# Tile 0's expert search taken head by head, in a fused attention, state-space and retrieval layer

## The reference

```
q = (rmsnorm(x) @ w_query)                      # 8 heads x 2 halves x 128
s = einsum('thcd,hckd->thck', q, keys)          # 128 scores per head and half
top_s, top_i = top_k(s, 16)
cand_s = top_s[0][:, None] + top_s[1][None, :]  # 16 x 16 sums per head
best_s, best_j = top_k(cand_s, 16);  idx = cand_i[best_j]
gate = softmax(best_s)
act  = gelu(einsum('thkd,td->thk', u_table[idx], x))
y    = einsum('thk,thkd->td', gate * act, v_table[idx])
```

## Time and profile before

| | us |
|---|---|
| median of the runs | 3525.19 |
| the profiled execution | 3523.02 |
| its span | 3521.2 |
| PE busy | 2364.3 (67%) |
| DVE busy | 2222.2 (63%) |
| POOL busy | 1322.6 (38%) |
| ACT busy | 1010.7 (29%) |
| gathers (L1372) | 1088, 1140.92 MB, 79.8% of the DMA engines' span |

### The profile page before, as it was taken

The page is one execution under the profiler, slowest core; times in us unless marked ns, Lnnn a source line. Parts: engine busy times, 40 slices in busy tenths (PEclk is TensorE's granted clock), DMA queues, the critical chain, the costliest instruction groups (busy, mean ns, idle before and its releaser), DMA issues.

```text
span 3521.2 us, 35625 instructions
## 1 busy us (share of the span) xinstructions
PE 2364.3 (67%) x9377; PEld 967.5 (27%) x9377; DVE 2222.2 (63%) x5008; ACT 1010.7 (29%) x3384; POOL 1322.6 (38%) x1229
## 2 busy tenths in 40 slices
PE   6997654476568566856685677567756765676676
PEld 3554434142114111411141124113311321241121
DVE  5344235557856775687568656855795578568754
ACT  2121211232333223233322332232233323332222
POOL 0010300344444444434444444444444434444442
PEclk9998777797688778967896778678867886897799
DMA  4111241699999999999999999999999999999998
GB/s 159 57 55 53 50 161 54 286 412 415 385 392 421 415 385 400 412 412 388 408 416 406 390 405 417 398 385 421 417 388 399 417 407 384 415 419 417 390 422 346
DMA packets 192652, 1212.96 MB, mean 344 GB/s; under 512 B 28952, under 2 KB 35416, under 8 KB 51688
## 3 DMA queue, kind: packets, MB, share of 16 engines
q0 software_dynamic: 156672, 1140.92, 79.8%
q1 hardware_dynamic: 35416, 69.28, 5.7%
q10 hardware_dynamic: 320, 0.07, 0.0%
HBM read 1194.51 MB, written 15.55 MB: 344 GB/s over the span
## 4 chain that ended last, share of the span: by engine, by line
DMA 29%; PE 22%; DVE 16%; issue 12%; ACT 5%; POOL 2%; DVEq 0%; SPq 0%; POOLq 0%; ACTq 0%; PEldq 0%
DMA uv_ring<-in_uv_table,idx 28%; PE ACC L1790 13%; PE TQ L1745 7%; DVE uv_ring L1633 5%; DVE S L1597 2%; DVE picks L1598 2%; DVE S L1596 2%; POOL uv_ring L1372 2%; ACT dg L1466 1%; ACT dot L1459 1%; PE OP L1726 1%; DMA wq<-in_w_query 1%; ACT dot L1449 1%; DVE dot L1633 0%; DVE pos L1528 0%
## 5 line engine op out<-in xcount | busy, mean ns | idle before, releaser
L1790 PE MATMUL ACC<-uv_ring,dg 128*64 128x512 f32 x4352 | 1472.8, 788 | 919.0 <-ACT dg L1466 918.3
L1372 POOL DMA_INDIRECT uv_ring<-in_uv_table,idx x1088 | 1258.3, 1157 | 1807.0 <-PE ACC L1790 1357.0
L1633 DVE CUSTOM_DVE_ANT_0 uv_ring<-uv_ring,xn 128x1024 f32<-128x1024 f32 x1088 | 1325.0, 1226 | 791.7 <-DMA uv_ring<-in_uv_table,idx 728.9
L1790 PEld LDWEIGHTS ACC<-uv_ring,dg 128*64 128x64 f32 x4352 | 343.7, 167 | 1930.8 <-ACT dg L1466 1396.9
L1449 ACT ACTIVATE dot<-dot 128x2 f32<-128x2 f32 x544 | 110.5, 203 | 1749.2 <-DVE dot L1633 1748.9
L1466 ACT ACTIVATE dg<-stack,dot 128x64 f32<-128x64 f32 x1088 | 327.8, 341 | 53.0
L1745 PEld LDWEIGHTS TQ<-glu_and_queries,wq 128*128 128x128 f32 x2304 | 266.4, 194 | 66.3 <-issue 64.7
L1745 PE MATMUL TQ<-glu_and_queries,wq 128*128 128x128 f32 x2304 | 280.5, 280 | 1.4 <-DMA wq<-in_w_query 1.2
L1459 ACT ACTIVATE dot<-gate,dot 128x1 f32<-128x1 f32 x1088 | 261.2, 287 | 17.7
L507 PE MATMUL PJ<-w_in,xT 128*128 128x512 f32 (+1 forms) x432 | 158.7, 528 | 1.5 <-DMA w_in<-in_w_in 1.5
L507 PEld LDWEIGHTS PJ<-w_in,xT 128*128 128x128 f32 x432 | 82.9, 192 | 79.2 <-issue 74.0
(11 more groups left out here) (319 smaller groups left out, 1653.2 us busy)
## 6 DMA issues: line engine op xcount, KB each, us to landing
uv_ring<-in_uv_table,idx POOLq DMA_INDIRECT x1088, 10.8
glu_and_queries<-in_w_glu SPq DMA_DIRECT2D x9, 1024.0 KB, 17.1
wq<-in_w_query SPq DMA_DIRECT2D x1, 8192.0 KB, 33.1
xt<-in_x SPq DMA_DIRECT2D x9, 512.0 KB, 3.4
xr<-scratch_x SPq DMA_DIRECT2D x9, 512.0 KB
w_in<-in_w_in SPq DMA_DIRECT2D x2, 2048.0 KB, 10.8
xk<-in_x SPq DMA_DIRECT2D x8, 512.0 KB, 3.2
scratch_x<-xk SPq DMA_DIRECT2D x8, 512.0 KB, 2.6
```

What stands on the lines that cost most here:

```text
L1372: pool.indirect_dma_start(out=ring[:, s_ % RING, :], out_offset=None, in_=a["uv_table"], in_offset=bass.IndirectOffsetOnAxis(ap=idx[:, s_: ...
L1633: V.tensor_tensor_reduce(row, row, xn[:, g, :], 1.0, 0.0, ALU.mult, ALU.add, dot[:, s_:s_ + 1]).then_inc(dots, 1)
L1790: ins = nc.tensor.matmul(ACC[GT * g:GT * (g + 1), b, :], dg[:, n % DG, :], ring[:, n % RING, D + 512 * b:D + 512 * b + 512], start=False, ...
```

## The change

- Tile 0 is a turn of its own, `first`, outside of the loop, which now runs tiles 1 to 6.
- Of tile 0's preparation only heads 0 to 2 of the step list (to xn_next and its transposes) run as before. Queries and scores are taken head by head on PE and ACT, one head's copy beside the next one's matmuls. DVE takes head 0 through its pieces A (two best16 of 128), B (62 candidates and their search), C and C2 (the match, in quarters, and the exchange to idx), then A of heads 1 to 3, then D of head 0 (the gates), and then products. The other pieces stand behind products of tile 0: head e's B at slot 3, 11, 20, 29, 38, 52, 66 (e = 1 to 7), C two slots later, C2 three, D five; A of heads 4 to 7 at slots 10, 18, 27, 36.
- POOL waits in tile 0 for an index semaphore once a head, ACT for gates once a head, and ACT takes one Exp for each head.
- Tile 1's whole preparation and the steps (0,*) of tile 2 run in slots 3 to 127 of tile 0: two steps a slot in slots 3 to 18, then some 1.03 a slot.
- In all tiles the exchange of numbers and gates is made by DVE, eight instructions on 64 partitions at step (7,13), which is slot 109; the matmul of picks at (7,14) is gone.
- w_query is laid out by head and loaded in eight transfers of 1 MB, the first of them ahead of keys, place and spread; stack and g_fin come last.

```diff
+        def first_steps(s_):
+            lo = LEAD + KS
+            return max(0, 2 * (s_ - LEAD)) if s_ < lo else 2 * KS + (s_ - lo) * (NSLOT - KS) // (NSLOT - lo)
+            if turn == "first":
+                lo, hi = first_steps(s_), first_steps(s_ + 1)
+                return [(1 + i // NSLOT, i % NSLOT // KS, i % KS) for i in range(lo, hi)]
+        BEST_AT = {1: 3, 2: 11, 3: 20, 4: 29, 5: 38, 6: 52, 7: 66}
+        FIRST_HEADS = {at + n: (e, piece) for e, at in BEST_AT.items() for n, piece in ((0, "B"), (2, "C"), (3, "C2"), (5, "D"))}
+        FIRST_HEADS |= {10: (4, "A"), 18: (5, "A"), 27: (6, "A"), 36: (7, "A")}
...
+                sp.dma_start(wq[:, 0].rearrange("p k n -> p (k n)"), a["w_query"][0]).then_inc(wq_in[0], 16)
...
+                for e in range(1, EH):
+                    sp.dma_start(wq[:, e].rearrange("p k n -> p (k n)"), a["w_query"][e]).then_inc(wq_in[e], 16)
-                sp.dma_start(wq[:], a["w_query"].rearrange("(k p) n -> p k n", p=P)).then_inc(weights, 16)
...
+                        if turn == "first" and s_ % KS == 0:
+                            pool.wait_ge(first["idx"], s_ // KS + 1)
...
+                def first_gates(e):
+                    act.wait_ge(first["nmax"], e + 1)
+                    A(ex[:, e, :], best[:, e, :], ACT.Exp, bias=nmax[:, e:e + 1],
+                      accum_out=esum[:, e:e + 1]).then_inc(first["ex"], 1)
...
-                        k["picked"].mark(V.tensor_tensor(ex, ex, bcast(esum[:], KS, 2), ALU.mult))
+                            k["gate_ready"].mark(take_gates(0, EARLY // KS))
+                            k["idx_ready"].mark(take_picks(0, EARLY // KS))
...
+                def first_head(e, piece):
+                    head, i = slice(e, e + 1), 2 * (e % 4)
+                    if piece == "A":
+                        dve.wait_ge(first["S"], e + 1)
+                        for n in range(2):
+                            best16(top_v[:, e, n, :], top_i[:, e, n, :], S[:, i + n, :])
+                        dve.sem_inc(first["topped"], 1)
+                    elif piece == "B":
+                        dch_(V.tensor_copy(top_f[:, head], top_i[:, head]))
+                        dch_(V.tensor_scalar(top_f[:, head, 0, :], top_f[:, head, 0, :], float(KEYS), None, ALU.mult))
+                        pairwise(top_v[:, head], first_cand, ALU.add)
+                        dch_(pairwise(top_f[:, head], first_cid, ALU.add), True)
+                        best16(best[:, e, :], pos[:, e, :], first_cand[:, 0, :])
+                        V.tensor_copy(pos_f[:, e, :], pos[:, e, :])
+                        dch_(V.tensor_scalar(nmax[:, head], best[:, e, 0:1], -1.0, None, ALU.mult))
+                        dve.sem_inc(first["nmax"], 1)
+                    elif piece in ("C", "C2"):
+                        n = KS // 4
+                        for k0 in range(0, KS // 2, n) if piece == "C" else range(KS // 2, KS, n):
+                            dch_(V.tensor_tensor(quarter[:], bcast(place[:], n, 1), bcast(pos_f[:, e, k0:k0 + n], NCAND, 2),
+                                                 ALU.is_equal))
+                            dch_(V.tensor_tensor(quarter[:], quarter[:], first_cid[:].to_broadcast([P, n, NCAND]), ALU.mult))
+                            dch_(V.tensor_reduce(idx_f[:, e, k0:k0 + n], quarter[:], AX.X, ALU.add))
+                        if piece == "C2":
+                            take_picks(e, e + 1).then_inc(first["idx"], 1)
+                    else:
+                        dve.wait_ge(first["ex"], e + 1)
+                        dch_(V.reciprocal(esum[:, head], esum[:, head]))
+                        take_gates(e, e + 1).then_inc(first["gate"], 1)
...
+                for piece in ("A", "B", "C", "C2"):
+                    first_head(0, piece)
+                for e in range(1, 4):
+                    first_head(e, "A")
+                first_head(0, "D")
+                for s_ in range(LEAD):
+                    product(0, s_)
...
+                retrieve("first", 0)
+                with dve.Fori(1, PT - 1) as t:
```

More of the change, by code:

```diff
@@ L1451, in weigh @@
                 def weigh(t, s_):
-                    if s_ == 0:
+                    if isinstance(t, int) and t == 0:
+                        if s_ % KS == 0:
+                            act.wait_ge(first["gate"], s_ // KS + 1)
+                    elif s_ == 0:
                         k["gate_ready"].of(act, t)
@@ L1482, in retrieve @@
                             diagonal(t, s_)
-                            if prep := prepared(turn, t, s_):
+                            if turn == "first" and FIRST_HEADS.get(s_, ("", ""))[1] == "B":
+                                first_gates(FIRST_HEADS[s_][0])
+                            for prep in prepared(turn, t, s_):
                                 prepare(*prep)
@@ L1614, in take_early @@
[L1614 to L1619, removed]
+                        if isinstance(t, int) and t == PT:
+                            k["gate_ready"].mark(take_gates(0, EH, 1))
+                            k["idx_ready"].mark(take_picks(0, EH, 1))
+                        else:
+                            k["gate_ready"].mark(take_gates(0, EARLY // KS))
+                            k["idx_ready"].mark(take_picks(0, EARLY // KS))
@@ L1653, in retrieve @@
                 def retrieve(turn, t):
-                    turn_now[0] = t
+                    turn_now[0] = None if turn == "first" else t
                     for s_ in range(LEAD, slots_of(turn)):
                         product(t, s_)
-                        if s_ == KS - 4 and turn != "samples":
+                        if s_ == KS - 4 and turn in ("steady", "eighth"):
                             take_rest(t)
-                        if s_ == TAKE and turn != "samples":
-                            take_early(t + 1)
-                        if prep := prepared(turn, t, s_):
+                        if turn == "first" and s_ in FIRST_HEADS:
+                            first_head(*FIRST_HEADS[s_])
+                        for prep in prepared(turn, t, s_):
                             prepare(*prep)
@@ L1679, in _ @@
                             dve.wait_ge(bottom, 16 * 2)
-                        elif (h, j) == (3, 0):
-                            dve.wait_ge(weights, 16 * 6)
                         prepare(0, h, j)
[L1683 to L1689, removed]
+                for piece in ("A", "B", "C", "C2"):
[3 more added lines that the diff above has]
+                first_head(0, "D")
+                dve.wait_ge(weights, 16 * 2)
+                for s_ in range(LEAD):
+                    product(0, s_)
+                for n in ("topped_a", "topped_b", "nmax_done", "idx_ready", "gate_ready", "idx_rest", "gate_rest"):
+                    dve.sem_inc(k[n].sem, 1)
+                retrieve("first", 0)
+                dch.loop_begins(1)
+                with dve.Fori(1, PT - 1) as t:
                     retrieve("steady", t)
@@ L1758, in prepare, with first_queries, first_scores, spread_rows @@
                         k[f"s_{n}"].mark(ins)
[L1759 to L1766, removed]
-                    k["xn_done"].of(pe, t)
[L1769 to L1773, removed]
+                def first_queries(e):
+                    pe.wait_ge(wq_in[e], 16)
+                    if e >= 2:
+                        pe.wait_ge(first["qT"], e - 1)
+                    for i in range(2):
+                        for n in range(KD):
+                            ins = nc.tensor.matmul(TQ[:, e % 2, i * P:(i + 1) * P], wq[:, e, n, i * QH:(i + 1) * QH],
+                                                   xnT[:, n, :], start=(n == 0), stop=(n == KD - 1))
+                    ins.then_inc(first["q"], 1)
+                def first_scores(e):
+                    pe.wait_ge(first["qT"], e + 1)
+                    if e >= 2:
+                        pe.wait_ge(first["S"], e - 1)
+                    if e == 0:
+                        pe.wait_ge(keys_in, 16 * 3)
+                    for i in range(2):
+                        ins = nc.tensor.matmul(ZS[:, e % 2, i * KEYS:(i + 1) * KEYS], qT[:, 2 * (e % 4) + i, :],
+                                               keys[:, 2 * e + i, :], start=True, stop=True)
+                    ins.then_inc(first["s"], 1)
+                def spread_rows(t, g):
+                    k["xn_done"].of(pe, t)
+                    for b in range(2):
+                        ins = nc.tensor.matmul((OP, TQ)[g][:, b, :], spread[:, g, :],
+                                               xn_next[:, 512 * b:512 * b + 512], start=True, stop=True)
+                    k[f"xn_spread_{'ab'[g]}"].mark(ins)
                 def begin(t):
@@ L1811, in _ @@
                 pe.wait_ge(early, 48)
-                for h in range(EH):
+                for h in range(3):
                     for j in range(KS):
@@ L1815, in _ @@
                             pe.wait_ge(bottom, 16 * 2)
```

(19 more changed lines are left out.)

123 lines of the change are left out of this document (83 added, 40 removed).

## The result

The changed kernel takes 3501.37 us (3497.77 to 3503.19), a ratio of 0.9928 [0.9914, 0.9943] to the kernel before: 24 us faster by the medians, where 52 were forecast. The profiled execution has a span of 3495.9, 25.3 less than before. Of the executions used further down, one with useless work early took 4522.55 us; it is in no ratio, and without it that kernel's median is 3516.95 and not 3517.28.

A forecast was written before the change was run, and what follows sets the result against it. DMA was taken to bound the experts' stage, with tile 0's search an idle hole before it. First product 81 us earlier, less 27 excess in tile 0, less 4 for the handover, gave 50: forecast 3473 us, range 3446 to 3503.

The forecast's parts named there:

- the sum was 54 us at product 128: Tile 0: first product 81 us earlier, less 27 us of excess up to product 128, a gain of 54.
- the term of DVE's idle time: Tile 0: 84.4 us of added DVE work set against 107 us idle, 28 of it after slot 80.
- First product 81 earlier: Before tile 0's products: head 0 alone goes first, so the first product comes at 566.7 against 647.91.
- Second half of xn by 567.5: Start of tile 0: the copy of the second group of rows ends by 567.5, before product 1 needs it.
- Slots 3 to 18, 19 over: Tile 0: 9 us work excess plus 12.5 of waits for PE and ACT (bounds 0 and 25), less 2.5 overlap.
- Slots 19 to 49, 4 over: Tile 0: 37.3 us of added DVE work against 36.4 idle; 4 us taken as excess.
- Slots 50 to 80, 4 over: Tile 0: 19.6 us of added DVE work against 19.4 idle; 4 us taken as excess.
- After slot 81, none: Tile 0 from slot 81: time as before, 127.8 us.
- The +4 for the handover: Seven tiles and the samples: exchange moved from slot 116 to 109, about 0.7 us a tile slower, +4 in all.
- That ACT's table loads are hidden: Tile 0: 14 table loads, 18 us on ACT, hidden by the ring's cycle: cost 0, or 5 us.
- The rival of stalls at double pace, 3500: Tile 0: double-pace preparation stalls PE, ACT and DVE, 25 us, pieces cost 10 in each later stretch; 3500, chance 0.10.

The follow-up runs named there:

- useless work early: Changed kernel plus 32 useless DVE comparisons of 248 elements, two behind each product of tile 0's slots 19 to 34: 3517.28 us, ratio 0.9976.
- even pace: Changed kernel with tile 0's 144 preparation steps spread evenly, 1.15 a slot over slots 3 to 127, not two a slot in 3 to 18: 3485.13 us, 0.9891.
- The two kernels with useless work: Changed kernel plus 32 useless DVE comparisons in tile 0, behind products of slots 19 to 34 (3517.28 us, 0.9976) or 111 to 126 (3504.81 us, 0.9949).

## Why the prediction was wrong

The mechanism was right: the hole before the first gather closes, and DVE's search inside tile 0 gives part of it back. Its size was not: the sum was 54 us at product 128, measured were 26. (The step from there to 3473 has a slip of its own: 50 less than the median of 3525.2 is 3475.) The step that failed is the term of DVE's idle time: it was taken as span less busy, and as larger still. By steps:

- **First product 81 earlier: 77.6.** I read the row of 128 query matmuls in the earlier trace rows as 16 groups of eight. It shows two records for each matmul, so it holds four heads of 16, and a head takes 3.74 us, not 1.8. Head 0's took 5.57, with the granted clock at 0.67 of full speed from 536.2 to 541.8. Pieces A to D of head 0 took 26.9 us with the pieces A of heads 1 to 3 between them, for 25.7 forecast; the instructions of a quarter took 0.42 us, 0.45 from start to start, as forecast.
- **Second half of xn by 567.5: 580.** The same error eight times over: a head takes PE 4.75 us, not 3. The wait of 8.6 made products 0 to 3 take 12.1 us. Before they took 8.2: 3.9 lost.
- **Slots 3 to 18, 19 over: 23.7.** The three waits were 6.5, 2.7 and 5.8 for 5 to 6, 2.5 and 4.5. This was the step best foreseen, and even pace shows that it counts in full.
- **Slots 19 to 49, 4 over: 10.9.** I named no wait here, though step (2,6) waited 3.1 for OP before too; here it took 4.5, and rows 6.6.
- **Slots 50 to 80, 4 over: 15.7.** The step that failed most. I took span less busy time, 79.0 - 59.6, as time that a piece can use. But tile 1's searches are there, and a search of 128 holds DVE 1.98 us, of which 1.57 are busy (first line below): nothing entered the gaps of its five chained instructions. 31 products at 1.15 and 15.5 searches at 1.98 are 66.3 of 80.2: 13.9 were free for 19.6 of work, and 3.9 and 4.8 of waits for S and rows came on top.
- **After slot 81, none: 2.7 won.**

Together 3.4 + 3.9 + 4.7 + 6.9 + 11.7 - 2.7 = 28. Nor is a product counted as 1.22 + 0.08 in the busy time, for which I had added 5 us of idle time to each stretch: three in a row after the change, from 580.18 to 583.62, are busy 3.44 of 3.44 us. The view of before held a better measure of free time, DVE's waits for rows in the stretches of the earlier trace rows. A window for DVE over one search, then these waits in 656.1:698.6, 698.6:778 and 778:857:

```profile
558.12:560.10 1.98, 1.57 (x9) 1.00 0.00 0
...
DVE uv_ring L1633 <- DMA uv_ring<-in_uv_table,idx: 18.6, 15, 2.6
DVE uv_ring L1633 <- DMA uv_ring<-in_uv_table,idx: 33.9, 26, 2.1
DVE uv_ring L1633 <- DMA uv_ring<-in_uv_table,idx: 9.4, 15, 1.4
```

Idle time was 19.4, 36.4 and 19.4 there: only in the last stretch is it twice the waits for rows. Added work less these waits is 28.2 - 18.6, 37.3 - 33.9 and 19.6 - 9.4. With the new or longer waits of after (15.0; 1.4 for OP and 6.6 for rows; 1.6 for S and 4.8 for rows) this makes 24.6, 11.4 and 16.6, where 23.7, 10.9 and 15.7 were measured. The two kernels with useless work agree with that: work is free where DVE waits for rows, and costs nearly its length where it doesn't.

The +4 for the handover can't be read from the changed kernel: its lead is 26.0 at product 128, 28.4 at product 256 and 25.3 at the end, and identical code of the later tiles varies by 13 from profile to profile. Alone the exchange did cost, but the stated reason isn't supported. That ACT's table loads are hidden held, to 3 us, and no run shows the search held by the ring or by PE's clock of 0.71 to 0.79. The rival of stalls at double pace, 3500, is nearest to the total, with 54 us over where 51.5 were measured, but that is in part luck: it had 34 in slots 3 to 18, which took 23.7, and 20 in the two later stretches, which took 26.6, and it missed 3.4 at the first product and 3.9 at the second.

## What to carry to other kernels

Time that an engine has free beside a stream of transfers is not span less busy: take its waits for the stream, stretch by stretch. Or price each piece by start to start in a row where it stands in a chain, add the products by theirs, and compare with the rate of the transfers. When work is moved beside a stream, halving the distance between a step and the one that waits for it can cost the whole latency once the engine has no slack, as in slots 3 to 18 here; spreading the steps evenly was worth more (12.4 us of tile 0, 13 by the ratios) than any other single edit that keeps all of the work. Count what a record is before dividing a group of them.

## What had not been expected

An fp32 matmul left two records here: 32 records stand for the 16 query matmuls of a head, in 3.74 us at a granted clock of 1.00. Some 12 to 13 us of useless DVE work in the gather stage lengthened its stretch by 1.0 us in one place and by 11.7 in another of the same tile.
